# A two-stage transformer kernel on one core: gate sums into the attention scores as one fp32r product, two thin projections joined into one, six tiles of each norm summed on VectorE

## The reference

```python
xn = rms_norm(h, attn_norm[i])
gq, gk, gv, gr, glr, fq, fk, fv, ff = jnp.split(xn @ w_in[i], cuts, axis=-1)
log_a = log_sigmoid(glr @ w_alpha_up[i] + b_alpha[i]) / 16     # glr: 16 columns, low rank
log_f = log_sigmoid(ff + b_forget[i])                          # ff: 8 columns, one per head
# forgetting attention, 8 heads of 64:
c = cumsum(log_f, over tokens)
logits = q k^T / 8 + c_t - c_s, causal; softmax; times v
h = h + concatenate([o_gla, o_fox]) @ w_out[i]
h = h + conv_ffn(rms_norm(h, ffn_norm[i]), ...)
```

## Time and profile before

| what | value |
|---|---|
| median of 3 runs | 1428.15 us (1422.39 to 1431.5) |
| the profiled execution | 1421.26 us, span 1419.5 us |
| TensorE busy, share of the span | 1301.7 us, 92% |
| VectorE | 926.3 us, 65% |
| ScalarE | 743.5 us, 52% |
| GpSimd | 138.0 us, 10% |
| the chain that ended last | TensorE 58%, VectorE 19%, ScalarE 7%, DMA 7%, issue 6% |
| mean granted clock of TensorE | 0.940 |

### The profile page before, as it was taken

How to read it: one execution, slowest core, us unless ns; L and a number is a source line. 1 busy time by engine, 2 the same in 40 slices (tenths; PEclk the granted TensorE clock), 3 DMA queues, 4 the chain that set the end, 5 groups by cost and what they waited for, 6 DMA issues and landing times.

```text
span 1419.5 us, 21349 instructions
## 1 busy us (share of the span) xinstructions
PE 1301.7 (92%) x8400; PEld 1140.4 (80%) x8400; DVE 926.3 (65%) x1393; ACT 743.5 (52%) x1043; POOL 138.0 (10%) x155
## 2 busy tenths in 40 slices
PE   7999998999999999989999998989768999999993
PEld 4888788999997888788999998975757777777773
DVE  4444447878544453458888446645477999999994
ACT  4433445455433333445455435514346888888883
POOL 4000000000000000000020000000000222222220
PEclk9999899999999899799999998966969999999997
DMA  9443336777553433336774553700214999999992
GB/s 261 145 134 121 102 97 170 208 210 213 178 172 108 145 105 118 119 90 178 224 215 150 188 175 118 178 33 1 89 60 139 351 359 362 350 359 357 356 358 91
DMA packets 209598, 262.16 MB, mean 185 GB/s; under 512 B 19775, under 2 KB 179051, under 8 KB 205019
## 3 DMA queue, kind: packets, MB, share of 16 engines
q1 hardware_dynamic: 196688, 232.99, 50.6%
q0 software_dynamic: 12448, 27.66, 6.1%
q10 hardware_dynamic: 363, 0.14, 0.1%
HBM read 257.61 MB, written 19.40 MB: 195 GB/s over the span
## 4 chain that ended last, share of the span: by engine, by line
PE 58%; DVE 19%; ACT 7%; DMA 7%; issue 6%; DVEq 1%; SPq 0%; POOLq 0%; ACTq 0%
PE ps L704 14%; PE ps L705 13%; PE ps L706 13%; DVE wlo L685 7%; DMA raw<-in_w_exp_up 6%; ACT whi L676 3%; PE ps L646 3%; DVE wlo_x L685 1%; PE ps L1885 1%; PE ps L1884 1%; DVE adr L767 1%; DVE Yb L1832 1%; DVE cv L1434 1%; PE ps L1941 1%; PE ps L774 1%
## 5 line engine op out<-in xcount | busy, mean ns | idle before, releaser
L685 DVE TENSOR_TENSOR wlo<-raw,whi 128x2048 fp32r<-128x2048 f32 (+1 forms) x186 | 420.2, 2264 | 163.0 <-ACT whi L676 161.9
L704 PE MATMUL ps<-xhi,whi 128*128 128x272 f32 (+2 forms) x1264 | 375.7, 297 | 45.2 <-DVE xlo L700 19.4
L676 ACT ACTIVATE whi<-raw 128x2048 fp32r<-128x2048 f32 (+1 forms) x186 | 352.0, 1893 | 112.3 <-PE ps L706 74.6
L705 PE MATMUL ps<-xlo,whi 128*128 128x272 f32 (+2 forms) x1264 | 369.6, 292 | 0.0
L706 PE MATMUL ps<-xhi,wlo 128*128 128x272 f32 (+2 forms) x1264 | 368.7, 292 | 0.0
L704 PEld LDWEIGHTS ps<-xhi,whi 128*128 128x128 f32 x1264 | 247.5, 196 | 55.4 <-issue 44.6
L705 PEld LDWEIGHTS ps<-xlo,whi 128*128 128x128 f32 x1264 | 246.8, 195 | 0.8
L706 PEld LDWEIGHTS ps<-xhi,wlo 128*128 128x128 f32 x1264 | 246.6, 195 | 0.0
L915 POOL DMA_INDIRECT spread<-Yb,dest x35 | 84.3, 2410 | 320.4 <-DVE Yb L1832 307.2
L2228 PE MATMUL ps<-whi,xs_hi 128*128 128x512 f32 x280 | 112.5, 402 | 1.8 <-DVE wlo L685 1.8
L1078 ACT ACTIVATE cv<-ps,PC 128x272 f32<-128x272 f32 (+1 forms) x88 | 45.5, 568 | 130.2 <-PE ps L706 130.2
(11 more groups left out here) (387 smaller groups left out, 2204.6 us busy)
## 6 DMA issues: line engine op xcount, KB each, us to landing
raw<-in_w_up SPq DMA_DIRECT2D x88, 512.0 KB
raw<-in_w_exp_gate SPq DMA_DIRECT2D x70, 512.0 KB
raw<-in_w_exp_up SPq DMA_DIRECT2D x70, 512.0 KB
raw<-in_w_exp_down SPq DMA_DIRECT2D x35, 1024.0 KB
raw<-in_w_in SPq DMA_DIRECT2D x33, 1024.0 KB
ada<-in_w_ada POOLq DMA_DIRECT2D x48, 512.0 KB, 4.0
raw<-in_w_down SPq DMA_DIRECT2D x16, 896.0 KB
raw<-in_w_out SPq DMA_DIRECT2D x8, 1024.0 KB
```

Of the source, the lines that this page charges most:

```text
L676: act.activation(whi[SLOT[n]][:, 0:nk, :], raw[n % RAW][:, 0:nk, :], ACT.Copy).then_inc(s_w_hi.sem, s_w_hi.event(CHUNKS[n]))
L685: dve.tensor_tensor(wlo[SLOT[n]][:, 0:nk, :], raw[n % RAW][:, 0:nk, :], whi[SLOT[n]][:, 0:nk, :].bitcast(F32), ALU.subtract).then_inc(s_w_ ...
L704: pe.matmul(dst, ah, bh, start=first, stop=False, **kw)
L705: pe.matmul(dst, ah, bl, start=False, stop=False, **kw)
```

## The change

It makes three edits. (1) The scores: negc becomes an fp32r tile of 72 rows; rows 64 to 71 hold the rounded sum (ScalarE), rows 0 to 7 the rest (VectorE), and one product with sel, which is 1 in rows h and 64+h, adds both. (2) The 8 forget and 16 low-rank columns lie in one tile of 40 columns (16 of them zeros), and one product of 8 matmuls into bank 6 takes both. (3) For five norms (n2 of both layers, n1 of the second, nf and n3) VectorE sums the squares of tiles 0 to 5 into part_sum, and TensorE multiplies that sum and tiles 6 and 7: three averages in place of eight.

```diff
-        onesrow = sb("onesrow", [8, T])
+        onesrow = sb("onesrow", [40, T])
+        sel = sb("sel", [72, FOX_H], F32R)
...
-        wsm = sb("wsm", [P, DEPTH, KT, 24])
+        wsm = sb("wsm", [P, DEPTH, KT, 40])
...
-        bfo = sb("bfo", [8, DEPTH])
+        bfo = sb("bfo", [40, DEPTH])
...
-        fz, fl, negc = sb("fz", [8, T]), sb("fl", [8, T]), sb("negc", [8, T])
+        negc = sb("negc", [72, T], F32R)
...
+        m = [pq_at + 4 * 6 * T, late_end]
+        part_sum = sb("part_sum", [P, 2, T], at=m)
+        fz, fl = (sb(n, [40, T], at=m)[32:40, :] for n in ("fz", "fl"))
+        fc = sb("fc", [72, T], at=m)[64:72, :]
...
-                           (wsm[:, l, :, 16:24], wv[:, :, IN_AT["ff"]:IN_AT["ff"] + 8]),
+                           (wsm[:, l, :, 32:40], wv[:, :, IN_AT["ff"]:IN_AT["ff"] + 8]),
...
-                           (bfo[:, l:l + 1], A["b_forget"][l:l + 1, :].rearrange("l h -> h l"))]
+                           (bfo[32:40, l:l + 1], A["b_forget"][l:l + 1, :].rearrange("l h -> h l"))]
...
+        SUMMED = [("n2", 0), ("n1", 1), ("n2", 1), ("nf",), ("n3",)]
...
             n = SQ_NO[(key, i)]
             if n >= 4:
-                act.wait_ge(s_averaged.sem, s_averaged.after(*SQ_KEYS[n - 4]))
+                key_, i_ = SQ_KEYS[n - 4]
+                if key_ in SUMMED and i_ < 6:
+                    act.wait_ge(s_summed.sem, s_summed.after(key_, max(i_, 1)))
+                else:
+                    act.wait_ge(s_averaged.sem, s_averaged.after(key_, i_))
             w = STATS[STAT_NO[key]][3]
             act.activation(sq[:, n % 4, 0:w], src, ACT.Square, **k_).then_inc(s_squared.sem, s_squared.event(key, i))
 
+        def stat_sum(dve, key, i):
+
+            w = STATS[STAT_NO[key]][3]
+            tot = part_sum[:, 1 if key == ("n3",) else 0, 0:w]
+            one = lambda j: sq[:, SQ_NO[(key, j)] % 4, 0:w]
+            dve.wait_ge(s_squared.sem, s_squared.after(key, i))
+            if i == 1:
+                o = dve.tensor_tensor(tot, one(0), one(1), ALU.add)
+            else:
+                dve.wait_ge(s_summed.sem, s_summed.after(key, i - 1))
+                o = dve.tensor_tensor(tot, tot, one(i), ALU.add)
+            o.then_inc(s_summed.sem, s_summed.event(key, i))
...
+            first = 5 if key in SUMMED else 0
             if key == ("n3",):
...
-            pe.wait_ge(s_squared.sem, s_squared.after(key, i))
-            pe.matmul(sum_bank(key)[:, 0:w], ones[:, :], sq[:, SQ_NO[(key, i)] % 4, 0:w],
-                                          start=(i == 0), stop=(i == n - 1)).then_inc(s_averaged.sem, s_averaged.event(key, i))
+            if i == 5 and key in SUMMED:
+                pe.wait_ge(s_summed.sem, s_summed.after(key, 5))
+                src = part_sum[:, 1 if key == ("n3",) else 0, 0:w]
+            else:
+                pe.wait_ge(s_squared.sem, s_squared.after(key, i))
+                src = sq[:, SQ_NO[(key, i)] % 4, 0:w]
+            pe.matmul(sum_bank(key)[:, 0:w], ones[:, :], src,
+                                          start=(i == first), stop=(i == n - 1)).then_inc(s_averaged.sem, s_averaged.event(key, i))
...
+            fill(wsm[:, :, :, 16:32], 0.0)
+            fill(negc[:, :].bitcast(F32), 0.0)
+            fill(sel[:, :].bitcast(F32), 0.0)
...
-                        act.activation(fl[:, :], fz[:, :], ACT.Abs).then_inc(s_fl_steps.sem, s_fl_steps.event("fl1", l))
+                        act.activation(fl, fz, ACT.Abs).then_inc(s_fl_steps.sem, s_fl_steps.event("fl1", l))
                         act.wait_ge(s_fl_steps.sem, s_fl_steps.after("fl1", l))
-                        act.activation(fl[:, :], fl[:, :], ACT.Exp, scale=-1.0).then_inc(s_fl_steps.sem, s_fl_steps.event("fl2", l))
+                        act.activation(fl, fl, ACT.Exp, scale=-1.0).then_inc(s_fl_steps.sem, s_fl_steps.event("fl2", l))
                         act.wait_ge(s_fl_steps.sem, s_fl_steps.after("fl2", l))
-                        act.activation(fl[:, :], fl[:, :], ACT.Ln, bias=1.0).then_inc(s_fl_steps.sem, s_fl_steps.event("fl3", l))
+                        act.activation(fl, fl, ACT.Ln, bias=1.0).then_inc(s_fl_steps.sem, s_fl_steps.event("fl3", l))
+                        act.wait_ge(s_lf.sem, s_lf.after("summed", l))
+                        act.activation(negc[64:72, :], fc, ACT.Copy).then_inc(s_fl_steps.sem, s_fl_steps.event("hi", l))
...
-                        dve.wait_ge(s_small_ff.sem, s_small_ff.after(l))
-                        dve.tensor_scalar(fz[:, :], ps[7][0:8, 64:64 + T], bfo[:, l:l + 1], None, ALU.add).then_inc(s_fz.sem, s_fz.event(l))
+                        if l == 0:
+                            dve.wait_ge(s_consts.sem, s_consts.after("first"))
+                            for r0 in (0, 64):
+                                dve.tensor_copy(sel[r0:r0 + 8, :], ident[r0:r0 + 8, r0:r0 + 8])
                         dve.wait_ge(s_small_glr.sem, s_small_glr.after(l))
                         dve.tensor_copy(glr1[0:16, :], ps[6][0:16, 0:T]).then_inc(s_glr.sem, s_glr.event(l))
+                        dve.tensor_scalar(fz, ps[6][32:40, 0:T], bfo[32:40, l:l + 1], None, ALU.add).then_inc(s_fz.sem, s_fz.event(l))
                         if l == 0:
                             dve.wait_ge(s_bc.sem, s_bc.after())
                             dve.tensor_copy(bc44[:, :], ps[6][:, 0:44]).then_inc(s_bc44.sem, s_bc44.event())
                         dve.wait_ge(s_fl_steps.sem, s_fl_steps.after("fl3", l))
-                        dve.scalar_tensor_tensor(fl[:, :], fz[:, :], 0.0, fl[:, :], ALU.min, ALU.subtract).then_inc(s_lf.sem, s_lf.event(l))
+                        dve.scalar_tensor_tensor(fl, fz, 0.0, fl, ALU.min, ALU.subtract).then_inc(s_lf.sem, s_lf.event(l))
                         dve.wait_ge(s_lf.sem, s_lf.after(l))
-                        dve.tensor_tensor_scan(negc[:, :], onesrow[:, :], fl[:, :], 0.0, ALU.mult, ALU.subtract).then_inc(s_negc.sem, s_negc.event(l))
+                        dve.tensor_tensor_scan(fc, onesrow[32:40, :], fl, 0.0, ALU.mult, ALU.subtract).then_inc(s_lf.sem, s_lf.event("summed", l))
+                        dve.wait_ge(s_fl_steps.sem, s_fl_steps.after("hi", l))
+                        dve.tensor_tensor(negc[0:8, :], fc, negc[64:72, :].bitcast(F32), ALU.subtract).then_inc(s_negc.sem, s_negc.event(l))
...
+                    keys = [("n2", l)] if kind == "out" else [("n1", l + 1)] if l + 1 < DEPTH else [("nf",), ("n3",)]
+                    for j in (2 * i - 2, 2 * i - 1):
+                        for key_ in keys if j >= 1 else []:
+                            stat_sum(dve, key_, j)
                     product_done(dve, g)
                     for t in range(2):
...
-                        pe.matmul(ps[4][0:qn, a:a + end], ident[0:8, h:h + 1].broadcast_to([8, qn]), negc[:, 0:end], start=False, stop=False)
+                        pe.matmul(ps[4][0:qn, a:a + end], sel[:, h:h + 1].broadcast_to([72, qn]), negc[:, 0:end], start=False, stop=False)
...
                         for k in range(KT):
-                            o = pe.matmul(ps[7][0:8, 64:64 + T], wsm[:, l, k, 16:24], XN[:, k, :], start=(k == 0), stop=(k == KT - 1))
-                        o.then_inc(s_small_ff.sem, s_small_ff.event(l))
-                        for k in range(KT):
-                            o = pe.matmul(ps[6][0:16, 0:T], wsm[:, l, k, 0:16], XN[:, k, :], start=(k == 0), stop=(k == KT - 1))
+                            o = pe.matmul(ps[6][0:40, 0:T], wsm[:, l, k, :], XN[:, k, :], start=(k == 0), stop=(k == KT - 1))
                         o.then_inc(s_small_glr.sem, s_small_glr.event(l))
                         if l == 0:
                             pe.wait_ge(s_glr.sem, s_glr.after(l))
+                            pe.wait_ge(s_fz.sem, s_fz.after(l))
                             pe.matmul(ps[6][:, 0:44], ones_1[0:1, :], rows44[0:1, :], start=True, stop=True).then_inc(s_bc.sem, s_bc.event())
...
-                        for t in range(2):
-                            stat_average(pe, ("n2", l), 2 * i - 2 + t)
+                stat_average(pe, ("n2", l), 5)
...
-                    if i:
-                        for t in range(2):
-                            stat_average(pe, key, 2 * i - 2 + t)
-                            if l == DEPTH - 1:
-                                stat_average(pe, ("n3",), 2 * i - 2 + t)
-                for t in range(2):
-                    stat_average(pe, key, 6 + t)
+                for i in (5, 6, 7):
+                    stat_average(pe, key, i)
                     if l == DEPTH - 1:
-                        stat_average(pe, ("n3",), 6 + t)
+                        stat_average(pe, ("n3",), i)
```

More of the change, by code:

```diff
@@ L342, in build @@
         s_squared = signal("squared")
+        s_summed = signal("summed")
         s_w_used = signal("w_used")
@@ L378, in build @@
         s_bc = signal("bc")
-        s_small_ff = signal("small_ff")
         s_small_glr = signal("small_glr")
@@ L633, in stat_average @@
```

(12 more changed lines are left out.)

## The result

| | before | after |
|---|---|---|
| median (lowest to highest) | 1428.22 us (1422.39 to 1431.5, 4 runs) | 1408.85 us (1406.56 to 1414.23, 4 runs) |
| profiled execution, span | 1421.26, 1419.5 us | 1406.56, 1404.5 us |
| TensorE busy, mean granted clock | 1301.7 us, 0.940 | 1281.6 us, 0.935 |
| VectorE, ScalarE busy | 926.3, 743.5 us | 937.0, 744.3 us |

The ratio is 0.9874 with a 95% interval of 0.983 to 0.9917: faster by 12 to 24 us, most likely by 18. I forecast 1404 us (24.5 us less), and 1408.85 lies in my range of 1390 to 1413. The rest of this text asks where each of the 24.5 us went, since the two profiled executions differ by only 15.

A forecast was written before the change was run, and what follows sets the result against it. It took TensorE to bound "in" and "down", with waits for wlo the next candidate. Scores 11.5, thin products 6.2 and norms 6.8 us sum to 24.5, taking the median from 1428.15 to 1403.7 us; range 1390 to 1413.

The forecast's parts named there:

- scores, 16 heads: Score product with negc as one fp32r pass, 0.21 us at 272 columns, 0.16 at 144: 0.72 us a head, 11.5 in all.
- thin product, layer 1: In "in", one chain of 8 matmuls replaces two of 3.67 us; 0.6 goes into waiting for fz, 3.0 us gained.
- thin product, layer 2: In "in", one 3.67 us chain goes; a wait for wlo takes 0.4 to 0.5, leaving 3.2 us.
- three norms at 272 columns: Between gemm groups, 4 averages of 0.46 us leave TensorE's path for each of three norms: 5.5 us gained.
- nf and n3: Two norms in "down" of layer 2: of 3.4 us removed, only 1.3 gained, since VectorE's adds delay the next wlo.
- rival (a): In the scores, the narrow fp32r product costs what fp32 does: 20.0 us saved, 1408 us; chance 0.20.
- (d): In the scores, the product with 72 rows is no faster than fp32: 13 us saved, 1415 us; chance 0.07.
- the new wait for wlo: In layer 2's "in", after the thin product, TensorE waits 0.4 to 0.5 us for the next chunk's wlo.
- the slip: In "down" of layer 2, VectorE's adds delay the residual adds by about 0.2, 0.85 and 0.85 us.
- (b): In "in", TensorE's four falls to 1.2 GHz may stay out, 12 us more saved: 1392 us; chance 0.14.
- (c): In "in", without the fp32 products the clock falls at more heads, 3.4 us each, 12 more falls: 1445 us; chance 0.06.
- rival (e): Waits for wlo take all of the norms' gain and layer 2's thin-product gain: 14.5 us saved, 1414; chance 0.07.

The follow-up runs named there:

- experiment 3: Only the norms edit (VectorE sums the squares of tiles 0 to 5) on the kernel before: 1430.82 us, ratio 1.0005.
- experiment 8: The changed kernel with negc and sel as tiles of 128 rows in place of 72: one execution of 1406.28 us.
- experiments 1 and 2: Against the kernel before: the scores edit alone, 1415.6 us, ratio 0.9893; the thin-product edit alone, 1428.28 us, ratio 0.9951.
- experiment 6: Changed kernel with sums of squares ahead of VectorE's residual-step split, and both engines' splits ahead of the gate steps: 1393.99 us, ratio 0.9757; repeated, 1405.66 us.
- Experiment 7: On top of experiment 6, the small product goes to free columns of bank 7, without waiting for fz: 1398.45 us, ratio 0.9786; repeated, 1406.92 us.

## Why the prediction was right, point by point

Each number below is a difference of stretches at equal clock, or of stretches whose length the clock did not change.

| step | forecast | in the traces |
|---|---|---|
| scores, 16 heads | 11.5 | 10.2 |
| thin product, layer 1 | 3.0 | 2.8 |
| thin product, layer 2 | 3.67 - 0.4 to 0.5 | 3.64 - 0.72 |
| three norms at 272 columns | 5.5 | 1.51 + 1.50 + 1.83 = 4.84 |
| nf and n3 | 1.3 | 2.05 |
| sum | 24.5 | 22.8 |

The 2.8 holds where a stretch at half clock falls into group 0, as it did in the profile that I read (3.41 us from 23.67 on). In experiment 3, whose thin products are the old ones, none fell there: group 0 and the thin products took 14.56 us, and the changed kernel's 13.23 are only 1.3 less. The start of group 1 is then set by VectorE's list, which the change does not shorten. I did not see this in the rows, so a part of that term is luck.

**The scores** were right in mechanism and 11% too large. The single pass at 144 columns came, so rival (a) falls, and with it (d). With 272/2400 = 0.113 and 144/2400 = 0.060 for the passes, 0.11 to 0.12 us show beside them, where I took 0.10; that is 0.03 us a head. And the 16-column product is not nothing: 0.05 us dearer, 0.8 us over 16 heads. It could have been read off before: two fp32 records took 0.06 us there in all, so the 0.10 each that I took for a load did not hold at 16 columns.

The product with negc shows 0.11 us beside its pass with 72 rows and with 128 (experiment 8), while the gemm stream, 128 rows each time, runs at 0.126 us a product. The Trainium skill, page "TensorE: Matmul & The Clock Gate", Part 3, "The mechanism", says under what overlaps that a load does so only when its row group differs; that agrees with the first and not with the second. The text above that list, and Part 2 of the same page, "Step-by-step: what each phase is for", let a load go ahead into a background weight buffer too, which agrees with the second and not with the first. What makes the load hide in the one and show in the other is not settled by these runs.

**The thin product** of layer 1 behaved as written: glr, fz, the wait, the start. I had group 1 of "in" start 3.0 us sooner. It starts 1.75 us sooner in the trace (38.59 and 36.84), although group 0 itself started 1.08 later (22.53 and 23.61; TensorE waits 7.5 us for xs, the first load from memory, and 6.8 before). So the stretch is 2.8 shorter. In layer 2 the new wait for wlo came where I put it and is 0.72 in place of 0.4 to 0.5: experiments 1 and 2 show that either edit alone does not bring it, and experiment 6 that moving the splits takes it away.

**The norms.** "Down" of layer 1 gave 1.83, as forecast (1.84). In "out" I read the idle time ahead of the residual add for one add and took it that two of 0.49 us fit later. They would have, while the averages stood on TensorE: the later residual adds had 1.56 us of idle time then. With the averages gone the groups end sooner and 0.62 is left for 0.98 of adds, so each of two residual adds slips by 0.2 to 0.3 us. The removed work had been the cover of the added work. In "down" of layer 2 the slip was smaller than I had it (about 0.6 us in place of 0.85, since four adds take 1.43 and not 1.6), so its waits for wlo are 0.2 and 0.6 in place of 0.6 and 1.2. That step of the argument was right in place, and its price too high.

**The clock.** Rivals (b) and (c) said that the change moves the half-clock stretches. Half-clock time in a head stretch, summed from the clock records, was 12.4, 22.9, 19.5, 36.6, 20.0, 12.4, 19.3 and 36.7 us with the old products (mean 22.5, four executions) and 9.4 to 28.9 with the new (mean 20.5, 18 stretches of nine executions). So neither fewer nor more of them came with the change, and both rivals fall at their prices: the stretches move from execution to execution. At 0.45 us of time for 1 us at half clock, layer 1's head stretch, less that, comes to 135.2 in all four executions with old products and to 129.9 to 130.4 in the nine with the new, and layer 2's to 127.3 to 127.5 and 122.3 to 122.6: 5 us each, which is 8 x 0.64. (The 0.45 is the slope between the two profiles of before: 3.11 us more for 6.90 at half clock.) My count of half-clock stretches in "in" was four before and I forecast four; the first profile after has six, and it says nothing about the change. The four leave out the one of 10.24 us that ends each layer's head stretch (from 173.86 and from 593.70 on), and the 3.41 and 5.70 us at half clock in the two groups 0.

**Why 15, 18, 22.8 and 24.5.** The terms add up to 22.8 us. The profiled executions differ by 15, since the first profile of before was a favourable one. The third-layer attention took 79.8 us there, and 83.9 to 85.3 in nine of the twelve other profiles: 4.65 us of the gap. The heads of layer 1 give another 4.4 (22.1 us at half clock against 12.4), "up" of layer 2 gives 1.5, the first load 1.1. The other way, what comes after that attention took 2.6 us less, and the heads of layer 2 gained 1.1 more than their share. The forecast said that this execution lay 6.9 us below its median, and still carried the difference over unchanged.

A frame around all edits, from group 0 of layer 1 to the start of the third layer, takes 835.5 and 842.1 us in the two profiles of before, and 817.4 and 822.0 in the two of the changed kernel. Time at half clock in it is nearly the same, 66.4 and 80.1 against 68.3 and 79.5 us. The difference is 18.2 and 20.0 us, 19.1 on average, which fits the 18 of the times and is 3.7 under the sum. The terms leave out where the half clock falls: in the kernel before, more of it fell where TensorE would have waited anyway and cost nothing. Some 1.5 us of the 3.7 lie in "up", as told under rival (e). Whether the change moves these stretches, or chance did in two profiles each, is open. So the forecast was right in its mechanisms, with the scores 1.3 us too large, the norms at 272 columns 0.7 too large and the double norm 0.75 too small. That its 24.5 us stood for the time of the whole program was not right: its terms hold at equal clock, and the range had the room for the rest.

**Rival (e)**, that waits for wlo take part 3 and the gain in layer 2, came to 0.72 + 0.8 us of new waits out of its 10, so it falls. The waits for wlo rose by 4.1 us in the profile, but the largest new one, of 1.91 us, stands in "up" of layer 2, where nothing was edited:

```profile
628.69 0.36 PE L732 MATMUL ps<-xhi,whi 128*128 128x258 f32 x1 [1.91 <-DVE wlo L713]
```

In the kernel before the same wait is 0.56 us. It follows the first group of "up". Over all profiles it is 0.8 us or less where a half-clock stretch falls into that group, and 1.8 or 1.9 where none does: VectorE sets the next start there, and the wait shows what the slow stretch would have hidden. With the old norms the stretch of 3.41 us fell into this group in all eight cases (four profiles, two layers) and cost nothing. With the new norms it fell behind the group in five of eighteen, and there it costs 1.5 us: the second group of layer 2 took 7.32 us in place of 5.82.

## What to carry to other kernels

When work leaves the busiest engine, the idle time of the others that you read in the old trace shrinks by the same amount: fit added work into what is left, and let it stand where its engine waits for something else, as the adds do behind the squares and ahead of the split. An edit to a queue is judged best by the time between two instructions that frame it, at equal granted clock; the time of the whole program needed 12 runs to see 7 us, and did not see 7 us of another part at all. But check the sum of such terms with one frame around all of them: here it gave 19 us for 22.8, since a slow stretch costs nothing ahead of a wait and its full price elsewhere. Where an accumulator bank is shared, look at who must read it before the next product may write: the wait for fz was one of 2.9 us for 44 columns.

## What was not expected of the hardware

- One unchanged stretch of 324 matmul records, the attention of the third layer, took from 75.5 to 85.3 us in thirteen executions, with 37.8 to 66.6 us of it at 1.2 GHz. Experiment 7 had 75.50 and 75.47 us in its two profiles, and experiment 6 had 81.28 and 84.86.
- In the heads of both layers TensorE falls to 1.2 GHz for 3.41, 6.83 or 10.24 us at a time, also while it shows as busy throughout (10.24 us from 141.24 on in the changed kernel). A fall ahead of a wait for VectorE costs nothing: group 0 and the thin product of layer 1 take 13.23 us with one and without, and the wait is 1.36 or 2.86 us.
- The same kernel's median moved by 8 to 12 us between two sessions (1393.99 and 1405.66; 1398.45 and 1406.92), while the kernel before moved by 1.
- An fp32r product of 16 columns costs 0.11 us from start to start beside a load of other weights, where the fp32 one of two records cost 0.06. I have no explanation for the latter.
